# Projection pieces inside the attention loop, handed out by the size of the item

## The reference

```
xn = rms_norm(h, g1)
gq, gk, gv, gr, glr, dq, dk, dv = split(xn @ w_in)      # one projection of 3088 columns
h = h + concat(gla(gq, gk, gv, gr, glr), diff_attention(dq, dk, dv)) @ w_out
h = h + hier_moe(rms_norm(h, g2))                       # top-1 group, top-2 experts of 32
```

## Time and profile before

| | |
|---|---|
| runs | 1264.33, 1260.25, 1263.06 us; median 1263.06 |
| profiled execution | 1262.13 us, span 1260.3 us |
| PE busy | 1162.5 us (92%) |
| DVE busy | 890.6 us (71%) |
| ACT busy | 690.3 us (55%) |
| mean granted PE clock | 0.962 |
| attention, first to last scores | 195.98 to 436.46 us of the span |

### The profile page before, as it was taken

How to read it: one execution, slowest core, us unless ns; L and a number is a source line. 1 busy time by engine, 2 the same in 40 slices (tenths; PEclk the granted TensorE clock), 3 DMA queues, 4 the chain that set the end, 5 groups by cost and what they waited for, 6 DMA issues and landing times. The chain is left out here.

```text
span 1260.3 us, 17095 instructions
## 1 busy us (share of the span) xinstructions
PE 1162.5 (92%) x5875; PEld 875.0 (69%) x5876; DVE 890.6 (71%) x1310; ACT 690.3 (55%) x913; POOL 252.4 (20%) x324
## 2 busy tenths in 40 slices
PE   5989999889988779999669999999999999999993
PEld 4868887567766468888546777777777777777772
DVE  4434324655566467887658999999999999999881
ACT  5424204343543353343237777777777777777771
POOL 2212103321110021222341221221122122112100
PEclk9999999999999789999779999999999999999997
DMA  8030210200200243433479999999999999999941
GB/s 309 37 98 1 100 67 1 76 25 27 92 26 17 76 144 109 149 130 144 184 287 378 372 386 371 372 390 379 370 379 388 373 370 395 381 365 379 388 113 26
DMA packets 67426, 273.34 MB, mean 217 GB/s; under 512 B 13156, under 2 KB 19880, under 8 KB 42664
## 3 DMA queue, kind: packets, MB, share of 16 engines
q1 hardware_dynamic: 56744, 245.32, 50.5%
q0 software_dynamic: 7168, 20.98, 7.3%
q10 hardware_dynamic: 3456, 6.29, 1.3%
HBM read 248.44 MB, written 28.32 MB: 220 GB/s over the span
## 5 line engine op out<-in xcount | busy, mean ns | idle before, releaser
L1851 DVE TENSOR_TENSOR main_w_low<-w_raw,main_w_high 128x2048 fp32r<-128x2048 f32 x192 | 438.9, 2287 | 55.7 <-ACT main_w_high L1847 55.7
L1847 ACT CAST main_w_high<-w_raw 128x2048 fp32r<-128x2048 f32 x192 | 365.9, 1908 | 80.4 <-PE main_score L1865 52.6
L1777 POOL DMA_INDIRECT main_xg<-xn_dram,main_token x32 | 76.2, 2381 | 381.3 <-DVE main_token L1757 376.6
L1863 PE MATMUL main_pt<-main_w_high,main_xT_high 128*96 128x512 f32 x256 | 104.3, 408 | 1.2 <-DVE main_xT_low L2007 1.2
L1863 PE MATMUL main_score<-main_w_high,main_hT_high 128*96 128x512 f32 x256 | 103.2, 403 | 1.2 <-DVE main_hT_low L2019 1.2
L1863 PE MATMUL main_po<-main_w_high,main_xT_high 128*96 128x512 f32 x256 | 101.4, 396 | 2.8 <-DVE main_w_low L1851 2.8
L1865 PE MATMUL main_pt<-main_w_high,main_xT_low 128*96 128x512 f32 x256 | 102.8, 402 | 0.0
L1864 PE MATMUL main_pt<-main_w_low,main_xT_high 128*96 128x512 f32 x256 | 102.1, 399 | 0.0
L1865 PE MATMUL main_po<-main_w_high,main_xT_low 128*96 128x512 f32 x256 | 101.7, 397 | 0.0
L1865 PE MATMUL main_score<-main_w_high,main_hT_low 128*96 128x512 f32 x256 | 101.2, 395 | 0.0
L1864 PE MATMUL main_po<-main_w_low,main_xT_high 128*96 128x512 f32 x256 | 101.0, 395 | 0.0
(11 more groups left out here) (301 smaller groups left out, 2346.0 us busy)
## 6 DMA issues: line engine op xcount, KB each, us to landing
w_raw<-in_moe_w SPq DMA_DIRECT2D x192, 1024.0 KB, 10.4
slot_raw<-in_w_in SPq DMA_DIRECT2D x12, 1024.0 KB, 7.3
main_x<-in_x SPq DMA_DIRECT2D x8, 512.0 KB, 11.1
slot_raw<-in_w_out SPq DMA_DIRECT2D x4, 1024.0 KB, 6.3
main_hx<-in_x SPq DMA_DIRECT2D x8, 512.0 KB, 3.9
out<-main_hx SPq DMA_DIRECT2D x8, 512.0 KB, 2.6
xn_dram<-main_xn SPq DMA_DIRECT2D x8, 512.0 KB, 2.8
gr_dram<-main_stage ACTq DMA_DIRECT2D x8, 256.0 KB, 2.0
```

The costliest lines, as they stand in the source:

```text
L1777: nc.gpsimd.indirect_dma_start(xg[u][:], None, s["xn2_dram"], bass.IndirectOffsetOnAxis(token[u][:, 0:1], 0), bounds_check=bound["x"], oob ...
L1847: nc.scalar.copy(wh[slot(c, e)][:], raw[u][c // 2][:, c % 2, :]).then_inc(w_high, 1)
L1851: nc.vector.tensor_tensor(wl[slot(c, e)][:], raw[u][c // 2][:, c % 2, :], wh[slot(c, e)][:].bitcast(F32), ALU.subtract).then_inc(w_low, 1)
L1863: nc.tensor.matmul(out, x_hi, w_hi, start=start, stop=False)
```

## The change

The pieces of a step are now given by the item's query block: 8 for items 0 to 3, then 7, 7, 6, 5, 4, 3 and 2 for each following four. The sum is the same 168. The steps in which chunk 4's weights are converted are 1 and 2 instead of 3 and 5. Those of chunks 5 and 6 follow from where their predecessors end, by the same rule as before: chunk 5 in steps 8 and 10 (before 9 and 11), chunk 6 in steps 17 and 19 (before 20 and 22). Units end elsewhere: dq 3 to 6 in steps 0 to 3, dq 7 in step 5 (before: steps 1, 2, 3, 5, 6), and gv 7 in step 31 (before 30).

```
+FILL = (8, 7, 7, 6, 5, 4, 3, 2)
+
 def fill_plan():
 
-    pieces = KD * (len(UNITS) - AHEAD)
-    sizes = [6 if m < N - HD else 2 for m in range(N - 1)]
-    sizes[N - HD - 1] += pieces - sum(sizes)
+    sizes = [FILL[m // HD] for m in range(N)]
+    assert sum(sizes) == KD * (len(UNITS) - AHEAD)
     upto = [sum(sizes[:m + 1]) for m in range(STEPS)]
...
     for ch in (4, 5, 6):
         m = 0 if ch == 4 else next(m for m in range(STEPS) if CHUNK_END[ch - 2] - 1 in ended_in(m))
-        split_at[m + 3] = (ch, 0)
-        split_at[m + 5] = (ch, 1)
+        split_at[m + (1 if ch == 4 else 3)] = (ch, 0)
+        split_at[m + (2 if ch == 4 else 5)] = (ch, 1)
```

## The result

The changed kernel takes 1301.7 us in the median, the kernel before 1262.9: a ratio of 1.0307 (95% interval 1.0291 to 1.0324), 39 us slower. A fourth execution took 1515.1 us at a mean granted clock of 0.73 and is left out as a slow one. The forecast was 1289, range 1279 to 1298: the direction was right, the size too small by 13 us. The profiled execution has a span of 1300.6 us against 1260.3.

The account below looks back on a forecast made before the run. Early steps last as long as TensorE's work, late ones as the scores-maxima-exponentials loop; +18.8 (items 0 to 7) -1.2 -1.3 +0.4 +0 +10.2 (end) = +26.9 on 1262.1 gives 1289 us, range 1279 to 1298.

Parts of the forecast that it names:

- Bound and direction: Attention phase: early steps last as long as TensorE's work, late ones as long as the loop; slower, chance 0.95.
- The chain behind a dq unit: Steps 1 to 4: TensorE idles about 5, 4, 4 and 1.7 us before transposing dq units that end with the previous step.
- The hand-over: End of attention: gv 7 ends in step 31, so spill, b tile and factors come late and uncovered, +10.2 us.
- A full stretch costs half its length, 1.7 us: Behind long TensorE waits: a 3.4 us stretch at clock 0.50 costs 1.7 us while TensorE sets the pace.
- I charge three: Steps 1 to 3: one half-clock stretch each, making items 0 to 7 72.1 us against 53.2, +18.8.
- Step 20: Step after chunk 6's second conversion, in step 19: forecast 8.7 us, with 2.3 us of TensorE idle.
- Items 24 to 27: Loop 8.1 us each: 32.4 us if the clock holds, 37.5 if it falls each time; middle 35.0, +0.4.
- Longer chains: Rival: chunk 4's late conversion lengthens steps 2 and 3, or items 24 to 30 run at half clock; up to 1299, chance 0.15.
- The final spill: Rival: b tile and factors find slack, so only a few us of the end's 10.2 remain; 1279 to 1281, chance 0.10.
- The other side: Rival: a step lasts as long as TensorE's own work, finished dq units being ready in time; 1257, chance 0.05.
- The mutual exclusion of VectorE and GpSimd: Items 0 to 7: by the skill's rule two conversions start 1.0 us later each, sum 2 us higher; not adopted.
- The formula for one DMA: End: 2 us plus bytes over 436 GB/s gives 2.6 us spill, 2.3 tile, wait 2.3 us less; not adopted.

Follow-up runs that it names:

- experiment 6: Kernel before with pieces handed out by where TensorE waits: 4 or 5 mostly, 7 to 9 behind conversions, 6 late, none in item 31; 1241.2 us, ratio 0.9831.
- experiment 4: Kernel before with pieces shifted the other way: 5 in items 0 to 17, 6 in items 18 to 30, none in item 31; 1249.8 us, ratio 0.9884.
- experiment 3: Changed kernel with 12, 8, 8, 4 pieces in items 0 to 3 instead of 8 each; 1284.8 us, ratio 1.0159.
- experiment 8: Changed kernel with chunk 4 converted in steps 2 and 4 instead of 1 and 2; 1296.1 us, ratio 1.0260.
- experiment 1: Changed kernel with item 31's two pieces given to items 26 and 27, so gv 7 ends in step 30; 1283.8 us, ratio 1.0145.
- experiment 5: Changed kernel with 16 thrown-away products ahead of the transposition in each of steps 2 and 3; 1292.7 us, ratio 1.0220.
- experiment 7: Changed kernel with chunk 7's weights requested behind the first tile of the linear attention, not ahead of the last spill's wait; 1297.3 us, ratio 1.0276.
- experiment 2: Kernel before with chunk 4 converted in steps 0 and 4 instead of 3 and 5; 1264.2 us, ratio 1.0002.

## Why the prediction was right in direction and too small in size

- **Bound and direction: right.** Early steps last as long as TensorE's work, steps from item 20 on as long as the loop. With 4 pieces item 22 took 7.5 us, and with 3 items 24 and 25 took 8.15, against a forecast of 7.1 and 8.1. The 7.1 was read from item 20 without the 0.2 us until TensorE resumes; with TensorE hardly waiting, in experiment 6, items 20 to 23 took 7.29 to 7.73. Experiments 4 and 6 show the other side of it: pieces put into the late steps cost almost nothing (step 27 took 8.62 us with six, 7.90 with none) and save half clock.
- **The chain behind a dq unit: right.** The waits were 4.93, 4.16, 3.94 and 1.71 us, forecast 5, 4, 4 and 1.7. Experiment 3 shows that the place of the unit's end makes them, not the number of pieces, and experiment 8 shows the 2.05 us of a conversion in the chain.
- **The hand-over: right.** 10.2 us on VectorE as forecast; 11.3 in all. The other 1.2 is half clock: in the changed kernel and in experiment 1 it begins ahead of item 31's scores, and in experiment 5, with the same wait of 10.24 us, 0.8 us behind their start; there the stretch took 20.15 us in place of 21.42. Experiment 1 removes the 10. The forecast said that the spill would share the DMA engines with the weights, and experiment 7 shows 2.4 us of that.
- **"A full stretch costs half its length, 1.7 us", "I charge three": the step that failed.** The forecast took each stretch as 3.4 us long; behind the long waits they were twice as long, 6.8 us (the rows of 0.50 above), and the clock over steps 1 to 3 was 0.77, 0.75 and 0.75. Three times 1.7 is 5.1 us; experiment 3 measured 7.6 by their absence. That and small lengths are the 3.6 us too few in items 0 to 7. Step 19 too lost 3 us (9.92, or 6.86 where the clock held), forecast 1.6. The trace of before already had one such stretch, which "each time followed by a stretch of 3.4 us" passed over. Behind a wait of 2.86 us step 30 took 12.15 us at 0.75, where step 29 had 10.50 at 0.83:

```profile
424.31:436.46 12.15, 9.15 (x37) 0.75 0.20 64
```
- **Step 20: mis-sized without the clock.** It was forecast at 8.7 and took 10.39 in all runs with these sizes, also where the clock held in step 19. I had let the spill and the conversion of step 19 begin before the step's end. But step 19 is bound by its loop, so its last exponential ends just where step 20's scores begin; spill, conversion, maxima and exponentials all lie behind one another in step 20 (the spill's copy begins at 361.18, the last exponential ends at 371.59). Steps 19 and 20:

```profile
351.52:361.44 9.92, 9.89 (x39) 0.67 0.00 0
361.44:371.83 10.39, 6.43 (x37) 0.99 0.07 27
```

  This 1.7 us, 1.4 of step 19, 0.2 of step 21 and 1.0 of steps 22 and 23 make the 4.4 us between forecast and measurement in items 16 to 23.
- **Items 24 to 27: the middle was taken, two of four steps fell.** 8.15, 8.16, 9.98 and 10.20 us against 35.0 in all, 1.5 too few.
- **Outside the attention: +3.8 us that no step names.** The code up to the first scores is the same, and these came between 194.4 and 198.9 us in the profiles with no relation to the edit. The profile of before was near the early end, that of the changed kernel at the late one. Without these 2.9 us the kernel would still stand at some 1299, outside the range. How much of it is chance, and why this kernel's three repeats agreed to 1 us, stays open.
- **The sum.** Of the 13.4 us between forecast and measured difference of the spans, 6.6 are half clock (2.5 in front, 1.4 in step 19, 1.5 in items 24 to 27, 1.2 in item 31), 1.7 are step 20, 3.8 lie outside the attention, and the rest are lengths of some tenths each, less 1.2 for items 28 to 30.
- **Rivals.** "Longer chains" came nearest by its half-clock part, with 1299 as its end, 3 us short. The final spill was not hidden. The other side, that a step lasts as long as TensorE's own work, is refuted by the first four waits. The mutual exclusion of VectorE and GpSimd that the Trainium skill gives ("SBUF — State Buffer", "SBUF: two separate sides") would have added 2 us. It did not hold back the conversions: that of step 2 began at 222.81 under the root of 222.12 and took its usual 2.29, and the wait was 4.16, at the forecast's own 4. The other way round something like it is in the trace: under the conversion of step 3 (236.22 to 238.51) a small GpSimd operation took 1.33 us in place of 0.23 and ended 0.1 behind it.

```profile
222.12 1.67 POOL L1149 TENSOR_TENSOR main_q_rs<-main_q_rs,minus_half 128x8 f32<-128x8 f32 x1
222.81 2.29 DVE L1277 TENSOR_TENSOR slot_low<-slot_raw,slot_high 128x2048 fp32r<-128x2048 f32 x1 [1.10 <-ACT slot_high L924]
...
237.28 1.33 POOL L1157 TENSOR_SCALAR main_o_rs<-main_o_ss 128x1 f32<-128x1 f32 x1
```

  The formula for one DMA that the forecast quotes from the Trainium skill ("DMA: Bandwidth & Descriptors", "Anatomy of one DMA — SWDGE (gpsimd) path") is given there for transfers that GpSimd issues. ScalarE and SyncE issue these. Its 2.6 us for the spill stand against 4.6 here and 2.1 in experiment 7; the sum did not use it.
- **Open.** Why step 19, behind the same wait of 3.0 us, took 9.9 us in the changed kernel (twice) and in experiment 1, 8.33 in experiment 7, which is equal up to there, and 6.86 in experiment 8, whose code differs in earlier steps. The runs show that the half clock behind a wait varies, not what decides it.

## What to carry to other kernels

When filler work is handed out in a loop, put it where the bound engine waits, read from the trace, and not where the items are small. Check at which place in a step each unit of it ends: a unit that ends with the step exposes its whole chain in the next one. The last unit's end decides when the next phase's loads may start, so it must not slip by a step. A wait of TensorE of the lengths seen here (2 to 5 us) is to be charged with the half clock that can follow it, 2.5 us each for the three long ones, and not with the stretch that happened to follow the last wait. A conversion queued ahead of the next maxima costs its time also where no dq unit ends: experiment 2 gained nothing.

## What the runs showed of the hardware

- Products whose results are thrown away made two steps 4.3 us shorter, with the granted clock at 1.00 instead of 0.75 (experiment 5).
- In the changed kernel the waits of 3.94 to 4.93 us each came with a stretch of 6.8 us at 0.50. In experiment 8 the wait of 3.94 us had one of 3.4 us (238.64 to 242.05), as the 3.72 us had before.
- A wait of 1.84 us (step 26) was followed by 0.50 in the changed kernel and not in experiment 7, whose code is equal up to there. A wait of 1.65 us in step 6 was in experiment 2 and not in the kernel before; one of 2.40 in experiment 4 and one of 3.00 in experiment 8 were not. Waits of 1.63 us and less never were in the attention of any run.
- A 256 KB spill landed in 2.1 us alone (experiment 7), in 4.6 beside 2 MB of weights, and in 6.4 and 6.6 in experiments 6 and 4, where it went out right behind the request for them.
